# Splitting each branch behind its predecessor, half of the last branch among the sample rounds, and a norm's factor applied after the first MLP product

## The reference

```python
h = rms_norm(x, n1)
z = h @ w_in                     # columns shared out among four mixers
# A: gated linear attention, B: HGRN2, C: multi-scale pooling, D: sparse attention
mix = sum(sigmoid(h @ w_gate[b] + b_gate[b]) * (o[b] @ w_branch[b]) for b in range(4))
x = x + mix @ w_out
x = x + relu(rms_norm(x, n2) @ w1) ** 2 @ w2
# rms_norm(x, g) = x * rsqrt(mean(x * x) + 1e-6) * g ; everything in fp32
```

## Time and profile before

| | us |
|---|---|
| median of 3 runs | 1477.59 |
| the profiled execution | 1469.0 |
| its span | 1467.2 |
| TensorE busy | 1328.6 (91%) |
| VectorE busy | 585.2 (40%) |
| ScalarE busy | 353.0 (24%) |
| GpSimd busy | 585.3 (40%) |

### The profile page before, as it was taken

The page is one execution under the profiler, slowest core; times in us unless marked ns, Lnnn a source line. Parts: engine busy times, 40 slices in busy tenths (PEclk is TensorE's granted clock), DMA queues, the critical chain, the costliest instruction groups (busy, mean ns, idle before and its releaser), DMA issues.

```text
span 1467.2 us, 23744 instructions
## 1 busy us (share of the span) xinstructions
PE 1328.6 (91%) x10332; PEld 1237.2 (84%) x10332; DVE 585.2 (40%) x965; ACT 353.0 (24%) x523; POOL 585.3 (40%) x437
## 2 busy tenths in 40 slices
PE   6799999996986989799988898986989999999999
PEld 5689999984785878677778887985989999999999
DVE  4233554534256444555554431305335520044200
ACT  4222121210251213233322111102332222122210
POOL 3424354211244236756342324303433554455542
PEclk9899999998997889899998999997999999999999
DMA  4211111004421224134232225203212322323323
GB/s 172 86 55 48 58 59 58 30 29 94 115 66 36 88 101 158 72 107 153 101 117 85 101 72 176 70 1 144 87 58 87 96 92 89 99 87 93 95 87 102
DMA packets 42909, 129.31 MB, mean 88 GB/s; under 512 B 3958, under 2 KB 15006, under 8 KB 40621
## 3 DMA queue, kind: packets, MB, share of 16 engines
q1 hardware_dynamic: 38197, 102.62, 21.5%
q0 software_dynamic: 4608, 25.17, 4.9%
HBM read 121.64 MB, written 6.36 MB: 87 GB/s over the span
## 4 chain that ended last, share of the span: by engine, by line
PE 83%; DVE 9%; DMA 3%; ACT 2%; issue 2%; POOL 1%; SPq 1%; DVEq 0%; ACTq 0%
PE PS L616 18%; PE PS L618 17%; PE PS L617 17%; PE PS L645 9%; PE PS L718 3%; PE PS L904 3%; PE PS L927 2%; DMA M<-w_tiles 2%; PE PS L913 2%; PE PS L607 1%; PE PS L1072 1%; PE PS L1060 1%; DMA M<-state_hgrn 1%; PE PS L872 1%; PE PS L755 1%
## 5 line engine op out<-in xcount | busy, mean ns | idle before, releaser
L2083 POOL TENSOR_TENSOR WL<-M,WH 128x512 fp32r<-128x512 f32 x318 | 427.8, 1369 | 735.6 <-ACT WH L1178 735.4
L616 PE MATMUL PS<-hH,WH 128*128 128x260 f32 x1360 | 405.4, 298 | 29.0 <-DVE M L1466 10.9
L617 PE MATMUL PS<-hL,WH 128*128 128x260 f32 x1360 | 392.7, 289 | 0.0
L618 PE MATMUL PS<-hH,WL 128*128 128x260 f32 x1360 | 392.5, 289 | 0.0
L616 PEld LDWEIGHTS PS<-hH,WH 128*128 128x128 f32 x1360 | 265.8, 195 | 35.1 <-issue 19.0
L1178 ACT CAST WH<-M 128x1024 fp32r<-128x1024 f32 x159 | 165.8, 1046 | 440.7 <-DMA M<-w_tiles 305.8
L617 PEld LDWEIGHTS PS<-hL,WH 128*128 128x128 f32 x1360 | 265.6, 195 | 0.3
L618 PEld LDWEIGHTS PS<-hH,WL 128*128 128x128 f32 x1360 | 265.2, 195 | 0.0
L618 PE MATMUL PS<-uH,WL 128*128 128x260 f32 x512 | 144.8, 283 | 0.0
L616 PE MATMUL PS<-uH,WH 128*128 128x260 f32 x512 | 144.7, 283 | 0.0
L617 PE MATMUL PS<-uL,WH 128*128 128x260 f32 x512 | 144.2, 282 | 0.0
(11 more groups left out here) (353 smaller groups left out, 2095.2 us busy)
## 6 DMA issues: line engine op xcount, KB each, us to landing
M<-w_tiles SPq DMA_DIRECT2D x159, 512.0 KB, 3.5
M<-x_T SPq DMA_DIRECT2D x8, 520.0 KB, 5.6
M<-cache_win_kv SPq DMA_DIRECT2D x2, 2048.0 KB, 10.3
y_T<-M SPq DMA_DIRECT2D x8, 260.0 KB
con<-tables SPq DMA_DIRECT2D x1, 1475.5 KB, 12.5
M<-state_gla SPq DMA_DIRECT2D x2, 512.0 KB, 9.0
M<-state_hgrn SPq DMA_DIRECT2D x2, 512.0 KB, 11.5
gla_sample<-M SPq DMA_DIRECT2D x2, 512.0 KB, 5.8
```

Of the source, the lines that this page charges most:

```text
L616: mm(out, hi[:, cols], x_hi, start=first, stop=False)
L617: mm(out, hi[:, cols], x_lo, start=False, stop=False)
L618: return mm(out, lo[:, cols], x_hi, start=False, stop=last_k)
L2083: last = p.tensor_tensor(WL8[s][:, c], WR[s][:, c], WH8[s][:, c], ALU.subtract)
```

## The change

- Splits: branch A is split in stage smp, when its last head is done (ScalarE at head step 9, VectorE behind head 7). Branches B, C and D (D's 512 prompt columns) are split right behind the last unit of the branch before. To make room, the upper part `BH` and the mix `mixT` change places (`BH` no longer lies where sample states are still being written out).
- Three of branch D's four weight tiles become half units of the filling, for the first 260 columns only (6 units of 12 matmuls); their evacuation multiplies by the gate and adds to the mix. Behind s6 six output tiles have only the second half left, the last two both halves. Only the 8 sample columns are split there. Weight buffers are shared out anew from tile 86 on.
- Second norm: the upper and lower part of x times the gain are made tile by tile behind the output projection, without the root. ScalarE squares, VectorE adds the squares up, and one product with ones makes the sum, behind the first two MLP tiles. The root multiplies the relu's output, before the square.
- GpSimd in s6: three stages of weight splits come before the first gathers; the second keys and the values are gathered together after the window's last product.

```diff
@@ -95,6 +95,7 @@
+T_LAST = T_D + 3
@@ -112,7 +113,7 @@
-    return halves
+    return halves + [("br", n, j, 0) for n in range(T_D, T_LAST) for j in range(2)]
@@ -139,7 +140,7 @@
-    return n % 4 if n < T_MIX else (n - T_MIX) % 3 if n < T_OUT else (3, 0, 1, 2)[(n - T_OUT) % 4]
+    return n % 4 if n < T_MIX else (n - T_MIX) % 3 if n < T_LAST else (3, 2, 0, 1)[(n - T_LAST) % 4]
@@ -194,7 +195,7 @@
-        if n >= T_D:
+        if n >= T_LAST:
@@ -219,7 +220,17 @@
-        SG_OF[_u] = FREED[_u - 2][1]
+        SG_OF[_u] = FREED[_u - 2 if _n < T_D else HALVES.index(("gate", T_GD + 2 * (_n - T_D) + _j, 0, _h))][1]
+def mix_unit(n, j):
+    if n >= T_D:
+        return 3, 2 * (n - T_D) + j
+    return (n - T_MIX) // 12, 2 * ((n - T_MIX) % 12 // 3) + j
+LAST_TANH = max(u for u in range(len(HALVES)) if HALVES[u][0] == "gate")
@@ -271,7 +282,7 @@
-        mL, BH = parts("mL", ZV0, KT), parts("BH", 28992, 4)
+        mL, BH = parts("mL", ZV0 + 4 * T, KT), parts("BH", ZV0, 4)
@@ -425,7 +436,7 @@
-        mixT = tiles(ZV0, KT)
+        mixT = tiles(ZV0 + 4 * T, KT)
@@ -475,6 +486,7 @@
+        D_HALVES = ((1,), (0, 1))
@@ -647,7 +659,7 @@
-                        b, d = (n - T_MIX) // 12, j
+                        b, d = mix_unit(n, j)
@@ -1083,6 +1095,7 @@
+            pe.wait_ge(sem("b_lo"), 17)
@@ -1090,9 +1103,7 @@
-                    if n == 0:
-                        pe.wait_ge(sem("b_lo"), 12 + c + 1)
-                    for h in range(2):
+                    for h in D_HALVES[n // 6]:
@@ -1110,10 +1121,7 @@
-                norm_sum("n2", n - 2, 6)
-            norm_sum("n2", 6, 6)
-            norm_sum("n2", 7, 6)
-            pe.wait_ge(sem("wo_ev"), 8)
+            pe.wait_ge(sem("wo_ev"), 6)
@@ -1121,7 +1129,11 @@
-                        in_step(t, "n2_h", hH, hL, (0, 2))
+                        in_step(t, "n2_h", hH, hL, (4, 6))
+                        pe.wait_ge(sem("n2_sum"), KT - 1)
+                        for h in range(2):
+                            last = mm(PS[:, 2 + h, 0:HALF], ones, half(RST, h), start=True, stop=True)
+                        last.then_inc(sem("n2_mm"), 1)
...
@@ -1186,8 +1198,9 @@
+                t = slice(0, T if b < 3 else L)
-                    nc.scalar.copy(BH[:, c], BR[b][:, c]).then_inc(sem("b_hi"), 1)
+                    nc.scalar.copy(BH[:, c, t], BR[b][:, c, t]).then_inc(sem("b_hi"), 1)
@@ -1205,21 +1218,19 @@
-                        if d == 0 and h == 1:
-                            if b == 0:
-                                act.wait_ge(sem("hn"), 8)
-                            else:
-                                act.wait_ge(sem("prod"), B_END[b - 1] + 1)
-                            if b == 2:
-                                act.wait_ge(sem("pool_ev"), 4)
-                            if b == 0:
-                                act.wait_ge(sem("st_out"), 128)
-                            branch_upper(b)
+                    if u in B_END:
+                        b = B_END.index(u) + 1
+                        act.wait_ge(sem("prod"), u + 1)
+                        if b == 2:
+                            act.wait_ge(sem("pool_ev"), 4)
+                        if b == 3:
+                            act.wait_ge(sem("ont"), 4)
+                        branch_upper(b)
...
@@ -1315,6 +1326,10 @@
+                if hh == 9:
+                    for c in range(4):
+                        act.wait_ge(sem("hn"), c + 1)
+                        nc.scalar.copy(BH[:, c], BR[0][:, c]).then_inc(sem("b_hi"), 1)
@@ -1376,28 +1391,28 @@
-            for n in range(T_D, T_D + 3):
-                upper(n)
+            upper(T_LAST)
-            act.wait_ge(sem("prod"), B_END[2] + 1)
-            branch_upper(3)
+            nc.scalar.copy(BH[:, :, L:T], BR[3][:, :, L:T]).then_inc(sem("b_hi"), 1)
-                if n in (2, 3, 5, 7):
-                    upper({2: T_D + 3, 3: T_OUT, 5: T_OUT + 1, 7: T_OUT + 2}[n])
+                if n in (2, 4, 6):
+                    upper(T_OUT + n // 2 - 1)
-                norm_square("n2", xN, k)
+                if k >= 3:
+                    act.wait_ge(sem("n2_sum"), k - 2)
+                f(SQN[k % 2] if k else RST, xN[:, k], ACT.Square).then_inc(sem("n2_sq"), 1)
-            norm_root("n2", 6)
-            h_upper("n2", {2: T_MLP + 3})
+            upper(T_MLP + 3)
+            norm_root("n2", 2, 1)
...
@@ -1446,19 +1461,22 @@
-                    b, d = (n - T_MIX) // 12, 2 * ((n - T_MIX) % 12 // 3) + j
+                    b, d = mix_unit(n, j)
-                    m = half(mixT[:, d], h)
+                    m, gate = half(mixT[:, d], h), half(TD[:, d] if b == 3 else TH[d % 2], h)
+                    rst = half(RST, j if b == 3 else h)
-                        v.scalar_tensor_tensor(m, half(TH[d % 2], h), 1.0, ps, ALU.add, ALU.mult)\
+                        if d == 5:
+                            dve.wait_ge(sem("st_out"), 128)
+                        v.scalar_tensor_tensor(m, gate, 1.0, ps, ALU.add, ALU.mult)\
-                        v.scalar_tensor_tensor(half(RST, h), half(TH[d % 2], h), 1.0, ps, ALU.add, ALU.mult)\
+                        v.scalar_tensor_tensor(rst, gate, 1.0, ps, ALU.add, ALU.mult)\
-                        v.tensor_tensor(m, m, half(RST, h), ALU.add).then_inc(sem("mix_add"), 1)
+                        v.tensor_tensor(m, m, rst, ALU.add).then_inc(sem("mix_add"), 1)
@@ -1467,17 +1485,19 @@
+                t = slice(0, T if b < 3 else L)
-                    v.tensor_tensor(BL[b][:, c], BR[b][:, c], BH[:, c], ALU.subtract).then_inc(sem("b_lo"), 1)
+                    v.tensor_tensor(BL[b][:, c, t], BR[b][:, c, t], BH[:, c, t], ALU.subtract)\
+                        .then_inc(sem("b_lo"), 1)
-                    elif n < T_GD and (n - T_MIX) % 12 == 0 and h == 1:
-                        branch_lower((n - T_MIX) // 12)
+                    if u in B_END:
+                        branch_lower(B_END.index(u) + 1)
@@ -1647,6 +1667,8 @@
+                if hh == 7:
+                    branch_lower(0)
@@ -2027,19 +2049,25 @@
-            branch_lower(3)
+            dve.wait_ge(sem("b_hi"), 17)
+            v.tensor_tensor(OL[:, :, L:T], ONT[:, :, L:T], BH[:, :, L:T], ALU.subtract).then_inc(sem("b_lo"), 1)
+                    hs_d = D_HALVES[n // 6]
+                    wide = slice(HALF * hs_d[0], T)
+                    parts_of = lambda ap: ap.rearrange("p (h n) -> p h n", n=HALF)
-                    dve.wait_ge(sem("sg"), FREED[P_D - 1][1])
+                    dve.wait_ge(sem("sg"), FREED[LAST_TANH][1])
-                    v.scalar_tensor_tensor(halves(RST), halves(TD[:, n]), 1.0, pair(2 * (n % 4)), ALU.add, ALU.mult)\
+                    v.scalar_tensor_tensor(parts_of(RST[:, wide]), parts_of(TD[:, n, wide]), 1.0,
+                                           PS[:, 2 * (n % 4) + hs_d[0]:2 * (n % 4) + 2, 0:HALF], ALU.add, ALU.mult)\
-                    v.tensor_tensor(mixT[:, n], mixT[:, n], RST, ALU.add).then_inc(sem("d_add"), 1)
+                    v.tensor_tensor(mixT[:, n, wide], mixT[:, n, wide], RST[:, wide], ALU.add)\
+                        .then_inc(sem("d_add"), 1)
@@ -2049,16 +2077,28 @@
-            dve.wait_ge(sem("wo_ev"), 8)
+                dve.wait_ge(sem("wo_ev"), n + 1)
+                if n == 0:
+                    dve.wait_ge(sem("prod"), P_D)
+                v.tensor_scalar(hH[:, n], xN[:, n], V("n2", n, n + 1), None, ALU.mult).then_inc(sem("n2_hi"), 1)
+                dve.wait_ge(sem("n2_hi"), n + 1)
+                v.scalar_tensor_tensor(hL[:, n], xN[:, n], V("n2", n, n + 1), hH[:, n], ALU.mult, ALU.subtract)\
+                    .then_inc(sem("n2_h"), 1)
+                if n:
+                    dve.wait_ge(sem("n2_sq"), n + 1)
+                    if n >= 2:
+                        dve.wait_ge(sem("n2_sum"), n - 1)
+                    v.tensor_tensor(RST, RST, SQN[n % 2], ALU.add).then_inc(sem("n2_sum"), 1)
-            norm_apply("n2", xN, "n2")
-                    v.tensor_tensor(US[r % 2], UR[r % 2], UR[r % 2], ALU.mult).then_inc(sem("u_sq"), 1)
+                    v.tensor_tensor(US[r % 2], UR[r % 2], RST, ALU.mult).then_inc(sem("u_rs"), 1)
+                    dve.wait_ge(sem("u_rs"), r + 1)
+                    v.tensor_tensor(US[r % 2], US[r % 2], US[r % 2], ALU.mult).then_inc(sem("u_sq"), 1)
...
@@ -2188,23 +2228,19 @@
-            for i in range(14):
+            for i in range(17):
-            for i in range(14, 27):
+            for i in range(17, 30):
-            gp.wait_ge(sem("sv_mm"), 4)
+            gp.wait_ge(sem("sv_mm"), 8)
-            tick("s6", 27)
-            gp.wait_ge(sem("sv_mm"), 8)
-            tick("s6", 28)
-            tick("s6", 29)
```

More of the change, by code:

```diff
@@ L1137, in _ @@
                         for h in range(2):
-                            last = triple(PS[:, 2 * (v % 4) + h, 0:HALF], t, 0, False, k, half(hH[:, k], h),
+                            last = triple(PS[:, 2 * ((v + 2) % 4) + h, 0:HALF], t, 0, False, k, half(hH[:, k], h),
```

(12 more changed lines are left out.)

## The result

The changed kernel takes **1431.18 us** (median of 4 runs, 1426.71 to 1435.17) against 1477.09 for the kernel before beside it: a ratio of 0.9694, 95% interval 0.9655 to 0.9733. A later set of the same kernel came to 1426.17 (5 runs, ratio 0.967 [0.9642, 0.9697]). The forecast was 1431, range 1422 to 1448. The profiled execution of after took 1428.43 us, with a span of 1426.6.

The account below looks back on a forecast made before the run. TensorE, 83% of the chain of waits, was taken to bound the kernel. Gains of 1.8 + 8.0 + 1.2 + 6.6 + 7.6 + 8.6 + 13.0 = 46.8 us off the 1477.6 median gave 1431, range 1422 to 1448.

Parts of the forecast that it names:

- The sum: All gains of the forecast added up over the whole kernel: 46.8 us saved.
- E: Second norm, from the output tiles to the MLP's first relu: 60.7 us become 47.2, less 0.5 charged, gain 13.0.
- D: Last branch: six units move into the sample rounds, shortening the block behind them from 192 matmuls to 120; gain 8.6 us.
- B: Second and third branch's splits move earlier; idles at their starts go, 2.5 us each paid at attention sums; gains 8.0, 1.2.
- A: First branch's split moves into the sample stage; TensorE's wait near 455 passes to an evacuation; gain 1.8 us.
- the third rival: Splits move but attention pays, a contended split taking 7.30 us: 1445 us; chance 0.16 together with another rival.
- C: Sample rounds: GpSimd's weight splits go ahead of the gathers, removing two TensorE idles; gains 6.6 and 7.6 us.
- lands no later than the first did, 9.0 us on: Before the last branch's block: the one weight tile behind the reload of x arrives 9.0 us after it.
- the 0.8: Before the last branch's block: the sample columns' cast, one subtraction and the hand-overs, estimated at 0.8 us.
- the three tight splits: MLP start: three weight tiles have one tile's time before use, about 0.6 us of slack; 0.5 charged in all.
- The slower rival: MLP: the VectorE-GpSimd lock makes weight splits the bound; a pair of halves at 6.8 us gives 1495; chance 0.03.

Follow-up runs that it names:

- the undone A: The changed kernel with the first branch's split put back at its old tick in the query and key norm: 1429.99 us, ratio 0.969.
- the early tile: The changed kernel with the last branch's remaining weight tile loaded ahead of the reload of x instead of behind it: 1421.82 us, ratio 0.9626.
- three multiplications: The changed kernel with the multiplication by the norm's factor done three times instead of once per tile of the MLP's first product: 1440.02 us, ratio 0.9768.
- with two: The changed kernel with the multiplication by the norm's factor done twice instead of once per tile of the MLP's first product: 1423.87 us, ratio 0.9657.
- the filled idle: The changed kernel with VectorE's two evacuations ahead of most norms and TensorE's next units ahead of the transposes, near 455 us: 1419.61 us, ratio 0.9627.

## Why the prediction was right, and where it wasn't

*The sum* held to within 3 us of 46.8 (44.0), with misses in both directions that partly cancel: +1.4 at the second branch and +0.9 in E, -3.7 in D. Taking it off the median and not off the profiled run was what made 1431 come out: the profiled run of before lay 8.6 us under it. That the first median met 1431 to the microsecond is luck; the later set of the same kernel came to 1426.17. No run undoes B as a whole, or D's six units: these two are read from the traces of before and after.

*A* was right in mechanism: the wait passed from the split to the evacuation, and the undone A costs nothing measurable. The size, 0.7 for 1.8, is below what can be told apart.

*B* paid its splits where it said, at the sums: the waits there grew by 1.8 and 2.1 us, against 2.5 taken. At the third branch the next wait grew too, from 4.5 to 6.24, so 1.2 became 0.15; that wait wasn't in the sum. The split took 2.5 at both new places, not the 7.3 of the third rival, which therefore didn't come.

*C* was right in both places.

*D* is the term that was mis-sized, 4.9 for 8.6. The step that failed is "lands no later than the first did, 9.0 us on" with the 0.8 behind it. The tile's cast came 10.3 us after the reload was issued (SyncE, then ScalarE, in after; the earlier trace rows have 991.31 and 1000.29), and the subtraction took 1.23 us beside GpSimd's split:

```profile
978.97 2.29 SPq L601 DMA_DIRECT2D M<-x_T  x4
```
```profile
989.28 1.04 ACT L1190 CAST WH<-M 128x1024 fp32r<-128x1024 f32 x1 [23.05 <-DMA M<-w_tiles]
```

So the block began 13.0 us after the last value product's reload and not 10.8; and the pushed matmuls cost 9.5 in the rounds and not 8.0. Of these 1.5 us, 1.0 is half clock, which no term had. Windows of the 10 us behind the last long idle of the rounds, before and then after:

```profile
957.45:967.45 10.00, 10.00 (x78) 9.41 (x79) 0.78 (x2) 0.96 (x2) 0.00 (x0) 0.74 0.01 2
```
```profile
935.62:945.62 10.00, 10.00 (x70) 9.31 (x71) 0.78 (x2) 1.52 (x2) 2.40 (x2) 0.64 0.17 52
```

The three traces without the six units have 0.72 to 0.75 there, the ten with them 0.63 to 0.72; why, and the other 0.5, is left open. I had counted one tile behind the reload as better than three and hadn't asked why any has to stand behind it; the early tile took 7.3 us off the idle, 4 to 9 off the medians.

*E* came out at 13.9 and 13.6 for 13.0: no matmul waited for the three tight splits, so the 0.5 charged for them wasn't needed. The estimate by the Trainium skill's rule ("SBUF — State Buffer", section "SBUF: two separate sides"), 11.1, was not borne out: the five pairs of halves that GpSimd made from 1040 to 1063 took 2.6 us each, and no matmul waited for them.

*The slower rival* was priced on the wrong engine. It let GpSimd's pair grow from 3.0 to 6.5 us; with three multiplications it grew by 0.06 and with two by 0.11 on the mean of the MLP. VectorE grows: its four instructions take 2.53 us undisturbed (0.70, 0.70, 0.43, 0.70) and 4.43 in after, and the limit on that side is 5.79. The real distance to a slower MLP was 1.36 us per tile: one more instruction fits, two don't.

## What to carry to other kernels

A wait that is removed is worth the distance to the next thing that is late on the engine that ends it: read that engine's order behind the removed instruction, and move the evacuation and not only the split; then look at the granted clock behind the place, which can take a part of the gain back. Budget an engine per tile with the durations that it shows beside its neighbour, not with its undisturbed ones. And before a block that waits for a transfer behind a bulk reload, ask whether that transfer could be issued ahead of it.

## What the runs showed of the hardware

**A GpSimd split holds a VectorE instruction for about 1.0 us, whatever its length.** Beside GpSimd's half splits, a VectorE instruction that is held grows by about 1.0 us: 0.19 to 1.23 (128x32 subtraction), 0.43 to 1.41 (cast), 0.70 to 1.67. So what VectorE loses depends on how many of its instructions meet a half. Per pair of halves it is 1.90 us with four instructions a tile (4.43 - 2.53), 1.90 with five (5.13 - 3.23) and 2.04 with six (5.97 - 3.93); in before, with three, almost only the subtraction is held, and it is 0.96 (2.79 - 1.83). GpSimd pays too, but less: in after its halves take 1.56 us on the mean from 1068 to 1153, where VectorE has these four instructions, and 1.31 from 1162 to 1250, where it has one per tile. The Trainium skill ("SBUF — State Buffer", section "SBUF: two separate sides") tells of an exclusive lock that whichever instruction starts first holds for its whole length. A later instruction that waits out most of a half agrees with VectorE's rows, and one that waits out the rest of a short VectorE instruction with GpSimd's; the order of the starts within a pair isn't shown here. The cast, with a single input, is held as well.

**The half clock behind an idle lasts differently long from run to run, and can begin without an idle.** An idle of 13.8 us ends near 356 in code that is the same in both kernels. Windows of before, then of after:

```profile
355.00:359.00 4.00, 3.52 (x18) 3.14 (x20) 3.26 (x7) 0.00 (x0) 0.00 (x0) 0.57 0.03 6
359.00:363.00 4.00, 4.00 (x32) 2.99 (x29) 1.99 (x4) 0.00 (x0) 0.00 (x0) 1.00 0.00 0
```
```profile
356.00:360.00 4.00, 3.18 (x14) 2.93 (x16) 3.59 (x7) 0.00 (x0) 0.00 (x0) 0.50 0.02 6
360.00:364.00 4.00, 4.00 (x19) 2.93 (x16) 1.39 (x2) 0.00 (x0) 0.00 (x0) 0.50 0.00 0
364.00:368.00 4.00, 4.00 (x26) 3.19 (x25) 1.41 (x3) 0.00 (x0) 0.00 (x0) 0.75 0.00 0
```

TensorE restarts at 355.48 and 356.82; the full level is back 3 us later in the one and 9 in the other. From the restart to 402.25 and 406.54, the same place in the code, pass 46.8 and 49.7 us. That is 2.9 of the 4.4 us by which the trace of after lags at 438; 1.3 are there before the restart. Over 356 to 371 the granted clock is 0.92 in before's profile, 0.67 in after's and 0.61 to 0.90 in the other eleven, so this one idle is worth up to 15 x 0.31 = 4.7 us.

Near 500 the clock falls to half while TensorE is busy, in before and in the three kernels with the filled idle. In the other nine traces the same stretch of code, up to the idle that ends at 515.92 in before, has a granted clock of 0.89 to 0.94 in place of 0.76 to 0.80. Windows of before, then of after:

```profile
502.00:508.00 6.00, 6.00 (x30) 5.77 (x28) 0.84 (x3) 2.71 (x3) 1.80 (x2) 0.50 0.51 175
```
```profile
502.00:508.00 6.00, 6.00 (x53) 5.82 (x52) 1.76 (x6) 0.00 (x0) 0.00 (x0) 1.00 0.28 77
```

In before no idle of over 0.7 us stands in the 20 us ahead of this fall. The stretch takes 35.8 us in before (480.14 to 515.92) and 33.3 in after, which is the +2.5 of the table. Why the clock falls there in some traces and not in others isn't shown.

So the two terms of the table that don't belong to the change are clock for the most part. For runs of one program one pair of traces tells: those of the changed kernel's two sets differ by 2.2 us in span, and by as much at 438 already. The runs of one program spread by 4 to 13 us here; in nine of the twelve sets the fastest run has the highest granted clock and the slowest the lowest, but where in the runs the rest of the spread lies isn't shown. A term of a few us is therefore read from a trace between two points, not from a difference of medians.
